# The weights of the seven products start 128 bytes, instead of 64, beyond all other matmul operands modulo 512 bytes

## What is computed

```python
def swiglu(h, w_in, w_out):
    gate, up = jnp.split(h @ w_in, 2, axis=-1)
    return (jax.nn.silu(gate) * up) @ w_out

# first block
f = (jax.nn.silu(h @ w_gate[l]) * (h @ w_up[l])) @ w_down[l]
```

## The kernel before

| tensor | start | modulo 512 |
|---|---|---|
| HH, HL | 32896, 49280 | 128 |
| WH0, WH1, WL0, WL1 | 76928, 82560, 88192, 93824 | 128 |
| ACCH, ACCL | 103552, 105600 | 128 |
| MEANR | 109056 | 0 |
| TH, TL | 109696, 208512 | 128 |
| M1H, M1L | 109696, 126080 | 128 |
| SH7 | 126144 | 192 |
| SL7 (and SUMS7, the same place) | 140480 | 192 |
| HEADMEAN, SQH, SQL | 202880, 158848, 160896 | 128 |
| VH, VL, and SH, SL of the retention | 134272, 194688, 223360, 189568 | 128 |

## Time and profile before

### The profile page before, as it was taken

How to read it: one execution, slowest core, us unless ns; L and a number is a source line. 1 busy time by engine, 2 the same in 40 slices (tenths; PEclk the granted TensorE clock), 3 DMA queues, 4 the chain that set the end, 5 groups by cost and what they waited for, 6 DMA issues and landing times.

```text
span 1927.9 us, 27809 instructions
## 1 busy us (share of the span) xinstructions
PE 1918.0 (99%) x9839; PEld 1607.4 (83%) x9839; DVE 1100.2 (57%) x1549; ACT 853.0 (44%) x1307; POOL 481.3 (25%) x187
## 2 busy tenths in 40 slices
PE   9999999999999999999999999999999999999999
PEld 6777889988888888888889998887777788999887
DVE  5775676665237455464276766323777677775500
ACT  6664644334234434434253344224667554343411
POOL 4223300003423343343410000443322240000343
PEclk9999999999999999999999999999999999999999
DMA  5112233223223222222232322222111132331332
GB/s 176 68 65 87 68 126 102 87 82 110 100 79 112 73 90 88 75 98 71 96 117 97 117 91 88 92 103 81 66 55 65 55 120 88 115 102 65 112 105 89
DMA packets 48880, 177.27 MB, mean 92 GB/s; under 512 B 5552, under 2 KB 6448, under 8 KB 48816
## 3 DMA queue, kind: packets, MB, share of 16 engines
q1 hardware_dynamic: 40032, 148.83, 22.4%
q10 hardware_dynamic: 8784, 27.59, 4.4%
HBM read 174.30 MB, written 2.10 MB: 91 GB/s over the span
## 4 chain that ended last, share of the span: by engine, by line
PE 95%; DVE 3%; ACT 1%; issue 1%; DMA 0%; SPq 0%; ACTq 0%; DVEq 0%
PE B L389 21%; PE B L390 21%; PE B L398 21%; PE B L860 4%; PE B L856 4%; PE B L858 4%; PE B L1185 1%; PE B L1189 1%; PE B L1186 1%; PE B L410 1%; PE B L415 1%; PE B L411 1%; PE B L1366 1%; PE B L1403 1%; PE B L1389 1%; PE B L1013 1%
## 5 line engine op out<-in xcount | busy, mean ns | idle before, releaser
L637 POOL TENSOR_TENSOR WL<-RAW,WH 128x1024 fp32r<-128x1024 f32 (+1 forms) x176 | 470.3, 2675 | 1420.7 <-PE B L398 1122.9
L370 ACT CAST WH<-RAW 128x1024 fp32r<-128x1024 f32 (+1 forms) x254 | 281.3, 1109 | 470.6 <-PE B L390 384.1
L389 PE MATMUL B<-HH,WH 128*128 128x512 f32 x1240 | 487.4, 393 | 0.9 <-DVE U L2136 0.4
L390 PE MATMUL B<-HL,WH 128*128 128x512 f32 x1240 | 483.8, 390 | 0.0
L398 PE MATMUL B<-HH,WL 128*128 128x512 f32 x1240 | 308.6, 391 | 0.0
L389 PEld LDWEIGHTS B<-HH,WH 128*128 128x128 f32 x1240 | 232.8, 188 | 50.3 <-issue 1.7
L390 PEld LDWEIGHTS B<-HL,WH 128*128 128x128 f32 x1240 | 233.1, 188 | 46.5
L398 PEld LDWEIGHTS B<-HH,WL 128*128 128x128 f32 x1240 | 229.3, 188 | 46.1 <-POOL WL L637 0.4
L389 PE MATMUL B<-MH,WH 128*128 128x512 f32 x440 | 171.2, 389 | 0.0
L390 PE MATMUL B<-ML,WH 128*128 128x512 f32 x440 | 171.2, 389 | 0.0
L2114 DVE TENSOR_TENSOR ACC<-ACC,SQ 128x512 f32<-128x512 f32 x38 | 74.6, 1963 | 112.1 <-ACT SQ L1492 111.9
(11 more groups left out here) (421 smaller groups left out, 3344.6 us busy)
## 6 DMA issues: line engine op xcount, KB each, us to landing
RAW<-in_w_small SPq DMA_DIRECT2D x208, 512.0 KB, 3.5
RAW<-in_w_large SPq DMA_DIRECT2D x48, 704.0 KB, 4.0
SUMS<-in_w_seven ACTq DMA_DIRECT2D x23, 512.0 KB, 4.1
R<-in_w_seven ACTq DMA_DIRECT2D x23, 512.0 KB, 3.5
out_t<-X SPq DMA_DIRECT2D x7, 256.0 KB, 4.9
X<-in_x_t ACTq DMA_DIRECT2D x4, 256.0 KB, 6.1
X<-in_x_t SPq DMA_DIRECT2D x4, 256.0 KB, 6.3
DECAY<-in_decay ACTq DMA_DIRECT2D x4, 256.0 KB, 2.6
```

The source lines that it names most:

```text
L370: act.copy(wh, raw).then_inc(s_hi, 1)
L389: pe.matmul(bank, wh[:, c, :], xh[:, k0 + c, :], start=(start and c == 0), stop=False)
L390: mm = pe.matmul(bank, wh[:, c, :], xl[:, k0 + c, :], start=False, stop=False)
L637: pool.tensor_tensor(wl, raw, wh.bitcast(F32), ALU.subtract).then_inc(s_lo, 1)
```

## The change

It changes four sizes of fillers. PHASE_SEVEN, ahead of SH7, grows from 16 to 32 elements of 4 bytes, and PAST_SL7 behind SL7 shrinks from 112 to 96, so that HD and everything behind it stays where it was. The second list, which lays SUMS7 over SL7, follows. SH7 now starts at 126208 and SL7 and SUMS7 at 140544, which is 256 modulo 512; the offset of lines 856 to 860 is 128.

```diff
@@ -177,11 +177,11 @@
         TH, _, SH7, SL7, _, HD, _, S3, TL, R = scratch([
-            ("TH", [P, 16, T // 2], F32R), ("PHASE_SEVEN", [P, 16]), ("SH7", [P, 28, P], F32R), ("SL7", [P, 28, P], F32R),
-            ("PAST_SL7", [P, 112]), ("HD", [P, FC, T]),
+            ("TH", [P, 16, T // 2], F32R), ("PHASE_SEVEN", [P, 32]), ("SH7", [P, 28, P], F32R), ("SL7", [P, 28, P], F32R),
+            ("PAST_SL7", [P, 96]), ("HD", [P, FC, T]),
             ("G1_SG_U1", [P, 3 * T]), ("S3", [P, 4, P]), ("TL", [P, 16, T // 2], F32R), ("R", [P, DC, P])])
         TB22, _, SUMS7, _, _, _, TSUM = scratch([
-            ("TB22", [P, 4, T // 2]), ("UP_TO_SL7", [P, 6 * T + 16 + 28 * P]), ("SUMS7", [P, 28, P]), ("UP_TO_HD", [P, 112]),
+            ("TB22", [P, 4, T // 2]), ("UP_TO_SL7", [P, 6 * T + 32 + 28 * P]), ("SUMS7", [P, 28, P]), ("UP_TO_HD", [P, 96]),
             ("HD_TILES", [P, FC * T]), ("G1_TO_S3", [P, 4 * T]), ("TSUM", [P, 16, T // 2])])
```

## The result

| | before | after |
|---|---|---|
| median of 22 runs each | 1929.79 us | 1933.99 us |
| after / before | | 1.0020, 95% interval 1.0015 to 1.0026 |
| profiled execution / its span | 1929.69 / 1927.9 us | 1933.69 / 1931.9 us |

The change costs 4.2 us by the medians, 0.20% by the ratio. It is slower, since the interval leaves out 1, but the interval holds the predicted bound of "no change" (0.2%, 3.9 us), so it isn't settled on which side of that bound it lies. The median is inside the predicted range of 1922 to 1946 and outside the likeliest case's own 1928.5 to 1930.9. Three of the 22 executions of each kernel were disturbed and took 4 to 6 us longer than the rest (1933.8 to 1935.2 before, 1937.9 to 1938.6 after).

The account below looks back on a forecast made before the run. PE, busy 99% of the span, was taken as the bound, so time is the sum of matmul start-to-start distances. The profiled 1929.7 us plus 0.0 for the products gave 1929.7 us, range 1922 to 1946.

Parts of the forecast that it names:

- likeliest case: Products in the three loops keep 117.2 to 118.4 ns each; 1928.5 to 1930.9 us, most likely 1929.7; chance 0.42.
- The preparation of the weights: ScalarE and VectorE work and loads into SUMS touching the moved tensors in the loops; hidden behind PE, costed at nothing.
- The one term: Change in start-to-start distance of the 1,932 products in the three loops, put at 0.0 us.
- forecast case: Products in the three loops stay unsettled at 117.2 to 118.4 ns; most likely 1929.7 us; chance 0.42.
- The run of 36: 36 products opening the first loop, 4.24 us before; the time expected after, 4.16 to 4.48 us, differed by case.
- case 1: Products in the loops stay unsettled as before, 117.2 to 118.4 ns each; most likely 1929.7 us; chance 0.42.
- case 2: Offset counts modulo 128 bytes; loop products return to a fixed pattern, 120.0 ns: 4.3 us more, 1934.0 us; chance 0.15.
- the named sign: Time of the 36 products opening the first loop: 4.24, 4.32, at most 4.16, or 4.48 us, depending on the case.
- refund of 2.4 us: Saving if 512-column matmuls behind the products need no settling, over 23 turns; would give 1931.6 us.
- Case 4: Loop products: plus 128 acts like minus 128, 6.7 ns each, 12.9 us more: 1942.6, at worst 1959.6 us; chance 0.22.
- the unsettled pace: Distance of 256-column matmuls in no fixed pattern: 117.8 ns at offset 64, 117.5 at offset 0 after an interruption.
- Case 3: Second 64 bytes gain as much as the first: loop products at 115.6 ns, 4.3 us less, 1925.4 us; chance 0.21.

## Why the prediction was right and where it failed

**What bounds the kernel** was right: matmul after matmul on PE, no wait for the products' weights before or after, and outside the three loops 0.13 us in all. The preparation of the weights, costed at nothing, cost nothing.

**That the offset counts, and not the address itself,** was taken for granted and was right: the kernel with everything 64 bytes later shows it.

**The one term failed in its size**: 0.0 us was put down for the products, at a pace of 117.8 ns that offset 64 and an unsettled stream at offset 0 have in common. It is 1.9 ns per product, 1,932 x 1.88 = 3.6 us, and 0.7 us at the entries. The step that failed is taking 117 to 118 for the pace of *any* stream that doesn't settle at offset 0. The ten offsets show no such common pace: the means go from 116.6 to 119.7 ns, and of the eight offsets that differ modulo 256 only 64 and 192 look alike within a run. The agreement that the step rested on was partly one of rounding: the eight distances of the earlier trace rows are 117.5 ns by the rows and 118.4 by the unrounded start times (117 to 121). The time fell into the range because the range was wide enough for four cases, not because the forecast case came.

**The signs.** The run of 36 was to take 4.24 us in case 1 and 4.32 in case 2. It takes 4.33 in the first turn of a loop and 4.28 in the others, so the named sign pointed to case 2 and the next turn to none. The products' mean, 119.65 ns, stayed just inside the 115.8 to 119.8 outside of which the forecast was to be wrong.

**The rivals.** Case 2 named the time, 1934.0 us, for a wrong reason, and that is luck. The offset doesn't count modulo 128: 0 and 128 differ in nearly every distance, and 64 and 192 differ in what follows a run. That both end at 119.6 ns is no common pattern. Its refund of 2.4 us does not exist, since the settling stands behind offset 0 as well. Case 4 comes nearest in its mechanism and had the wrong price. Modulo 256 holds for both pairs that were run (0 and 256, 64 and 320), so plus 128 should be minus 128, though offset 384 itself was not run: the changed kernel pays 0.64 us in all at its 92 entries, 232 to 235 ns where the matmul ahead of MEANR takes 232. But I took MEANR's 0.24 us for a price of the offset, 6.7 ns over the unsettled pace. All five pairs of lines 709 and 710 in the trace have it, 241 and 240 ns, but each is two matmuls of 512 columns in the middle of another stream, and that gives no pace for 36 matmuls of 256; it was 1.9 ns. Case 3, a second 64 bytes gaining as much as the first, is out; there is a gain left, but at 192 and 224.

**The rule of the Trainium skill** ("SBUF — State Buffer", "SBUF: two separate sides", by which PE never waits on anyone) has no room for any of this if it is read as the prediction read it, so that no offset matters: kernels that differ in an offset alone lie 6 us apart. But it speaks of engines that wait on one another, and no run here shows that PE waits on another engine. What holds what up is not shown: that the reads of the streamed operand and of the next weights get in each other's way is the natural reading of a dependence on the difference of their addresses, but it stays an argument.

**Chances.** "Slower by over 0.2%" had 0.29, "within 0.2%" had 0.50. The medians put the result 0.3 us over the bound, and the interval of the ratio holds the bound, so it can't be said which of the two came.

**What stays open:** why the rhythm of an offset is what it is, and so what offset would be best; and how the distance ahead of a run comes to decide, in the kernel with shifted plain weights, between 113.6 and 117.8 ns at the same addresses.

## What to carry to other kernels

Where PE is never idle, the distance between the starts of two matmuls is the thing to read, not their duration; a few ns of it, at thousands of matmuls, are microseconds, and in this kernel they depended on the start of the weights against the start of the streamed operand, modulo 256 bytes. Apart from the repeat after 256 bytes, no rule tried here told one offset from the others, so try all eight steps of 32 bytes (finer ones were not tried), for each width of stream if it can be done, and judge by the whole turn with the matmuls ahead and behind, since the cheapest products (224) were not in the fastest kernel (192).

## What was not expected of the hardware

- The dependence repeats after 256 bytes in both pairs that were run: 1933.34 and 1933.19 us at 0 and 256, 1929.6 and 1929.57 at 64 and 320.
- The 512-column matmuls behind a run of products cost 27 or 28 ns more than their settled pace (234, 236, 228, 232, 231 against 226.7 ns) behind every run of the kernel before, and at offset 0 too. It is no fixed price: 8 to 10 ns behind every run at offset 192, 9 to 34 in the changed kernel, 36 to 52 at offset 32. And it doesn't take a change of width: behind MEANR, with 512 columns throughout, they go 235, 233, 236, 224, 231, 236.
- The same code at the same addresses ran at 113.6 and at 117.8 ns a product in one execution, and which of the two goes with the one distance ahead of the run; 113.6 is the shortest mean of a run of 256-column matmuls in the traces read here.
